# The seventh down chunk of both feed-forward networks by seven block products, with its fold spread over GpSimd and VectorE, in a two-block transformer kernel

## What is computed

```
def first_block(x, ...):
    ...
    h = rms_norm(x, norm_mlp[l])
    x = x + jnp.square(jax.nn.relu(h @ w_up[l])) @ w_down[l]
    return rms_norm(x, norm_final)

def second_block(x, ...):
    ...
    n2 = rms_norm_2(h, norm_mlp_pre[l])
    hid = jnp.square(jax.nn.relu(jnp.einsum('bsd,df->bsf', n2, w_up[l])))
    mlp_out = jnp.einsum('bsf,fd->bsd', hid, w_down[l])
    h = h + rms_norm_2(mlp_out, norm_mlp_post[l])
```

## Time and profile before

| | |
|---|---|
| median of 3 runs | 1567.17 us (1567.06 to 1567.26) |
| the profiled execution's own time | 1567.51 us |
| span from its first to its last instruction | 1565.7 us |
| TensorE busy | 1549.0 us, 99% of the span |
| VectorE, ScalarE, GpSimd busy | 987.3, 662.7, 482.6 us |
| down6 / down7 of the first network on TensorE | from 717.07 us / from 738.83 us |
| down6 / down7 of the second network on TensorE | from 1515.58 us / from 1537.34 us |

### The profile page before, as it was taken

The page is one execution under the profiler, slowest core; times in us unless marked ns, Lnnn a source line. Parts: engine busy times, 40 slices in busy tenths (PEclk is TensorE's granted clock), DMA queues, the critical chain, the costliest instruction groups (busy, mean ns, idle before and its releaser), DMA issues.

```text
span 1565.7 us, 21038 instructions
## 1 busy us (share of the span) xinstructions
PE 1549.0 (99%) x7752; PEld 1303.1 (83%) x7752; DVE 987.3 (63%) x1188; ACT 662.7 (42%) x1092; POOL 482.6 (31%) x282
## 2 busy tenths in 40 slices
PE   8999999999999999999999999999999999999998
PEld 6888888888788888888888898988888988888886
DVE  5454876435477776876664747357356677777765
ACT  5352665244444443443533433643334453434342
POOL 2451000000037776752300000020013047767732
PEclk9999999999999999999999999999999999999999
DMA  6422136221313233215332132243334332213133
GB/s 247 150 70 79 41 108 191 79 81 54 135 54 108 108 108 107 107 55 160 89 106 83 55 95 71 92 162 105 111 124 147 135 108 102 89 45 135 67 116 120
DMA packets 44997, 164.35 MB, mean 105 GB/s; under 512 B 5584, under 2 KB 5784, under 8 KB 44272
## 3 DMA queue, kind: packets, MB, share of 16 engines
q1 hardware_dynamic: 40608, 144.82, 28.4%
q0 software_dynamic: 4304, 18.38, 3.4%
HBM read 158.89 MB, written 5.85 MB: 105 GB/s over the span
## 4 chain that ended last, share of the span: by engine, by line
PE 93%; DVE 4%; ACT 2%; DMA 1%; issue 1%; SPq 0%; DVEq 0%; ACTq 0%
PE banks L1235 29%; PE banks L1237 29%; PE banks L1236 29%; PE banks L1534 1%; PE banks L1413 1%; DVE nmax L2230 1%; DVE w_lo L1944 1%; DMA w_raw<-in_weights 1%; PE banks L1352 0%; PE banks L1596 0%; DVE banks L2229 0%; PE banks L1572 0%; PE banks L1564 0%; PE banks L1523 0%; DMA x_tok<-in_x 0%
## 5 line engine op out<-in xcount | busy, mean ns | idle before, releaser
L1235 PE MATMUL banks<-act_hi,w_hi 128*128 128x512 f32 (+1 forms) x1088 | 413.7, 380 | 3.1 <-DVE act_lo L2112 3.1
L1237 PE MATMUL banks<-act_hi,w_lo 128*128 128x512 f32 (+1 forms) x1088 | 410.3, 377 | 0.0
L1236 PE MATMUL banks<-act_lo,w_hi 128*128 128x512 f32 (+1 forms) x1088 | 410.2, 377 | 0.0
L1944 DVE TENSOR_TENSOR w_lo<-w_raw,w_hi 128x1024 fp32r<-128x1024 f32 x216 | 280.0, 1303 | 203.2 <-ACT w_hi L1632 199.8
L1632 ACT ACTIVATE w_hi<-w_raw 128x1024 fp32r<-128x1024 f32 x216 | 227.0, 1059 | 251.6 <-DMA w_raw<-in_weights 196.8
L1235 PEld LDWEIGHTS banks<-act_hi,w_hi 128*128 128x128 f32 x1088 | 204.9, 188 | 40.8 <-DVE w_lo L1944 1.6
L1237 PEld LDWEIGHTS banks<-act_hi,w_lo 128*128 128x128 f32 x1088 | 204.9, 188 | 37.7
L1236 PEld LDWEIGHTS banks<-act_lo,w_hi 128*128 128x128 f32 x1088 | 205.0, 188 | 36.4
L1235 PE MATMUL banks<-w_hi,a_hi 128*128 128x512 f32 x400 | 155.8, 389 | 0.0
L1237 PE MATMUL banks<-w_hi,a_lo 128*128 128x512 f32 x400 | 155.7, 389 | 0.0
L1236 PE MATMUL banks<-w_lo,a_hi 128*128 128x512 f32 x400 | 155.7, 389 | 0.0
(11 more groups left out here) (367 smaller groups left out, 2393.4 us busy)
## 6 DMA issues: line engine op xcount, KB each, us to landing
w_raw<-in_weights SPq DMA_DIRECT2D x216, 512.0 KB, 3.7
w_down<-in_weights SPq DMA_DIRECT2D x48, 512.0 KB, 6.4
wide<-share_dram POOLq DMA_DIRECT2D x3, 1024.0 KB, 10.2
x_tok<-in_x SPq DMA_DIRECT2D x4, 512.0 KB, 5.2
w_first<-in_weights SPq DMA_DIRECT2D x4, 512.0 KB, 8.5
x_tok<-in_x POOLq DMA_DIRECT2D x4, 512.0 KB, 5.0
x_dram<-x_tok POOLq DMA_DIRECT2D x1, 2048.0 KB, 8.1
x_tok<-x_dram POOLq DMA_DIRECT2D x1, 2048.0 KB, 8.5
```

The lines of the kernel that those rows point to most:

```text
L1235: pe.matmul(out_ap, lhs[0], rhs[0], start=start, stop=False)
L1236: pe.matmul(out_ap, lhs[0], rhs[1], start=False, stop=False)
L1237: return pe.matmul(out_ap, lhs[1], rhs[0], start=False, stop=stop)
L1944: dve.tensor_tensor(w_lo[:, slot, :], landed(kind, raw), w_hi[:, slot, :], ALU.subtract).then_inc(lo_w, 1)
```

## The change

- `seven(g)` now takes in down6: its weights come through `w_down`, and `tsum` runs for it.
- `run_mlp` runs down6 as `s.products(dst, last=True)`. "whole" moves ahead of it, so GpSimd makes `act_lo` for down7 while down6 runs. The ScalarE and GpSimd work on the next chunk's parts, which a down step by products has otherwise, falls away there.
- `fold` leaves VectorE in up7. Its parts follow the products from which they can be made: after products 1, 2, 3 and 4 on GpSimd (`fold_on_pool`: six operations of 128x1024 in the first network, five in the second), after product 6 on VectorE (two operations, which wait for GpSimd's third and fourth). GpSimd waits for its own last one before it goes on, and the adds of down7 to the last quarter wait for it too.
- `load2` and `unpark` stand behind "whole" and ahead of the fold in GpSimd's order, and wait for product 0 to be read.
- The parked residual comes back into `x_late`, which lies over `w_down`, and the output is written from there.

```
-    return name in ("w_down", "w_down_2") and row0 < FF - 2 * T
+    return name in ("w_down", "w_down_2") and row0 < FF - T
...
+        if last:
+            sums, held = None, self.count("lo_a", 4)
+            self.add("whole", held=held, sq=squared)
...
-        s.add("whole", held=s.count("lo_a", 1), sq=s.count("sq", 0), dst="parts")
-        up(after="fold")
-        after_last()
-        steps = s.bank_steps("add", "tok", "parts", rows=4, halves=2, dst=dst)
-        go(steps, 1)
-        s.add("whole", held=s.count("lo_a", 4), sq=s.count("sq", 0), dst="act")
-        go(steps, 16)
-        s.add("unpark", ready=ready(), dst=dst)
+        up()
+        for st in s.products(dst, last=True):
+            taken = filled_by(st)
+            if st.n == 0:
+                after_last(taken)
+                s.add("unpark", ready=taken, dst=dst)
+            s.add("fold", n=st.n, ready=taken, dst=dst)
         last(s.bank_steps("add", "tok", "act", rows=4, halves=2, dst=dst, by_tile=True))
...
             def fold(st):
+                at_ = FOLDS[st.dst]
+                q, (x11, x12, x21, x22) = sums_of[st.dst], quarters(st.dst)
+                if st.n == 6:
+                    wait_ready(dve, st.ready, None)
+                    dve.wait_ge(fold_made, at_ + 3)
+                    dve.tensor_tensor(x12, x12, q["q1"], ALU.add)
+                    dve.wait_ge(fold_made, at_ + 4)
+                    then(dve.tensor_tensor(x21, x21, q["q7"], ALU.add))
...
+                    if st.rows == 4 and st.nth >= TT // 2 and st.half == 1:
+                        dve.wait_ge(fold_made, LAST_FOLD[st.dst])
...
-                    pool.dma_start(x[:].rearrange("q t d -> q (t d)"), x_dram).then_inc(x_again, 16)
+                    wait_ready(pool, st.ready, turn)
+                    pool.dma_start(x_late[:].rearrange("q t d -> q (t d)"), x_dram).then_inc(x_again, 16)
...
+            def fold_on_pool(st):
+                at_ = FOLDS[st.dst]
+                q, (x11, x12, x21, x22) = sums_of[st.dst], quarters(st.dst)
+                if st.n in (1, 2, 3, 4):
+                    wait_ready(pool, st.ready, None)
+                if st.n == 1:
+                    pool.tensor_tensor(x11, x11, q["q1"], ALU.add).then_inc(fold_made, 1)
+                elif st.n == 2:
+                    pool.tensor_tensor(q["q6"], q["q6"], q["q1"], ALU.add).then_inc(fold_made, 1)
+                    pool.wait_ge(fold_made, at_ + 2)
+                elif st.n == 3:
+                    pool.tensor_tensor(q["q1"], q["q6"], q["q5"], ALU.add).then_inc(fold_made, 1)
+                elif st.n == 4:
+                    pool.tensor_tensor(q["q7"], q["q7"], q["q6"], ALU.add).then_inc(fold_made, 1)
+                    pool.wait_ge(fold_made, at_ + 4)
+                    if st.dst == "y":
+                        pool.tensor_tensor(x22, q["q7"], q["q5"], ALU.add).then_inc(fold_made, 1)
+                    else:
+                        pool.tensor_tensor(q["q5"], q["q7"], q["q5"], ALU.add).then_inc(fold_made, 1)
+                        pool.wait_ge(fold_made, at_ + 5)
+                        pool.tensor_tensor(x22, x22, q["q5"], ALU.add).then_inc(fold_made, 1)
+                    pool.wait_ge(fold_made, LAST_FOLD[st.dst])
```

More of the change, by code:

```diff
@@ L374, in ahead, with products @@
         return out
-    def products(self, dst, first=False):
+    def products(self, dst, first=False, last=False):
         g = self.group
@@ L398, in products @@
             ends.append((bank + 1, self.cell(self.fills[bank + 1] + 1, ("bank", bank + 1))))
-            yield self.add("product", banks, n=j, dst=dst, first=first, splits=splits,
+            yield self.add("product", banks, n=j, dst=dst, first=first, last=last, splits=splits,
                            units=[self.placed(self.mine[j])], held=held, of=ends, sum_a=sums, sq=squared)
@@ L763, in make_schedule @@
     s.gemm("up", "T", "act", ready=act_ready, pairs=True)
-    run_mlp("x", lambda: s.add("load2", ready=all_out()), first_end)
+    run_mlp("x", lambda taken: s.add("load2", ready=taken), first_end)
     go(s.project0, 16)
@@ L1152, in part_lo, with quarters @@
             eng.tensor_tensor(a_lo[:, j], parts[j], a_hi[:, j], ALU.subtract).then_inc(lo_a, 1)
+        def quarters(dst):
+            rows_of = {"x": x, "y": y}[dst]
+            return [rows_of[:, 2 * rows:2 * rows + 2, 512 * cols_:512 * cols_ + 512] for rows in range(2) for cols_ in range(2)]
         def copies_of(st):
@@ L1967, in gemm @@
                     split(st, turn)
-                if st.after == "fold" and st.bank == 0:
-                    fold(st)
                 b = st.bank
@@ L2030, in handle @@
                     split(st, turn)
+                elif k == "fold":
+                    fold(st)
                 elif k == "product":
@@ L2400, in handle @@
                     block_sums(pool, st, turn)
-                elif k == "product":
+                elif k == "product" and not st.last:
                     for j in (st.n - 1, st.n) if st.n == 6 else (st.n - 1,):
```

62 lines of the change are left out of this document (22 added, 40 removed).

## The result

The changed kernel takes 1578.45 us (median of 6 runs, 1577.73 to 1585.32), the kernel before 1567.22 us beside it. The ratio over all these runs is 1.0078, 95% interval 1.0063 to 1.0094: slower by 0.8% (the two medians alone give 1.0072, or 11.2 us). The profiled execution took 1577.73 us, the shortest of the six, and 10.2 us more than that of before.

A forecast was written before the change was run, and what follows sets the result against it. TensorE, at work for 1549.0 of 1565.7 us, bounds the kernel. +6.9 (tile 0's chain), +2.0 (clock) and -0.6 (second network) give +8.3: 1575.8 us profiled, 1575.5 us as median, range 1570.0 to 1578.5.

The forecast's parts named there:

- they take turns, a whole instruction each: On the SBUF port shared by VectorE and GpSimd, each waits for one whole instruction of the other; 6.4 us on GpSimd's fold.
- the term of the second network: Second network: -2.72 us for the saved step, +2.1 us for product 6 waiting for a bank; -0.6 us, tail unchanged.
- What bounds the kernel: TensorE, at work for 1549.0 of 1565.7 us; only shortening its stream or making it wait moves the time.
- the step saved: Each down6 loses one of eight steps, 12 matmuls, 2.72 us; 5.4 us for both networks.
- The rival without port waits: No waits for the port at all: fold done at R 25.7, -4.4 us, 1562.8 us, faster; chance 0.07.
- The chain of tile 0: First network: fold, split, row product, factor and scaling start tile 0's transposes 40.2 us after down6 starts, against 33.3; +6.9 us.
- The wait for `h_tok`: First network: TensorE finishes tile 1, then stands idle once for 8 to 10 us ahead of tile 0's transposes.
- The clock: Idling 8 us brings TensorE to 1.2 GHz before tile 0's transposes in the first network; +2.0 us, bounds 0 and 5.4.
- VectorE has the room to catch up: Second network's down7: tile 0's adds at about R 27 come in time, so the tail keeps its length.

The follow-up runs named there:

- e7: The changed kernel with all fold operations left out on GpSimd and VectorE, so the output is not the reference's: 1563.59 us, ratio 0.9977.
- e9: First network as before the change; second by seven products, residual fetch behind the third fold operation, third and fourth splits behind the next add, x21 moved: 1565.02 us.
- e5: The changed kernel with the whole fold on GpSimd waiting for the add of product 4 instead of starting product by product: 1579.07 us, ratio 1.0074.
- e1: The changed kernel with one wait added: GpSimd's second fold operation first waits until its own first one is done: 1574.49 us, ratio 1.0046.
- e4: The changed kernel with three edits: own wait, weight splits behind the adds, fold of tiles 2 and 3 behind row products of tiles 0 and 1: 1571.23 us.
- e6: The changed kernel with the step making act_hi and act_lo behind product 0, so GpSimd's transfers stand ahead of the act_lo operations: 1580.63 us, ratio 1.0085.
- e8: First network as before the change; only the second has the seventh chunk by products, with its fold from the add of product 4 on: 1568.98 us.
- e2: The changed kernel with VectorE's third and fourth weight splits of the last down step by products behind the next product's add: 1574.46 us, ratio 1.0046.
- e3: The changed kernel, first network only: GpSimd's fold operations 4 to 6 behind row products of tiles 0 and 1, x21 ahead of tile 2's adds: 1581.19 us.

## Why the prediction was right in direction and too low

The sum said +8.3; the profiled execution gave +10.2 and the medians +11.2. The step that failed is the rule for the port, "they take turns, a whole instruction each", and through it the term of the second network, -0.6 forecast and +2.55 measured. By the prediction's own terms:

- **What bounds the kernel, and the step saved: right.** Both down6 have 84 matmuls; e7 and e9 give -2.6 and -2.7 for one network where nothing else is in the way. The rival without port waits, -4.4, is what e7, without any fold, comes near to (-3.6).
- **The chain of tile 0: right, +6.4 instead of +6.9.** The fold ended at R 30.1, and x21, which the forecast had ahead of the fold's end, at 31.2 (31.8 forecast for both); the split behind it ended at 32.4 (33.0), the row product at 34.5 (35.0), the factor at 37.9 (38.3), and the transposes started at 39.75 (40.2). The failed step below left this chain alone: the hold made VectorE wait, and GpSimd, on which the chain hangs, went on (2.44 and 2.36 us for its first two operations).
- **The wait for `h_tok`: 2.87 us instead of 8 to 10.** The time was lost earlier: TensorE stood 4.0 us ahead of product 6 and took 2.5 more for it at the lower clock, and the chain of tile 0 was as late as before for all that. In e5, with no product wait, it was 11.3.
- **"They take turns, a whole instruction each": this step failed.** It is true where the GpSimd instruction behind the running one has no transfer ahead of it (and e9), and it was carried over to a place that has transfers directly ahead. There the split waits for two fold operations. In the second network the times ahead of it came as forecast: fold operation 1 started at R 10.6 (10.8 forecast) and the third split asked at 11.4 (11.3), but it ended at 16.4 instead of 14.3, 5.04 us instead of 3.0. In the first network, where the forecast had the same wait or none, the fourth split took 5.52 us. The Trainium skill (SBUF — State Buffer, "SBUF: two separate sides") gives the pair to whoever starts first, for the whole instruction; the trace agrees that it is whole instructions, but e1 to e4 and e6 show splits that asked first and still came behind operations that had not begun, for up to 7.86 us.
- **Second network, -0.6 forecast, +2.55 measured: the term that broke the sum.** It is -2.72 for the step, +3.57 for product 5 (due at 1536.83, started at 1540.40; the forecast had product 6, 2.1 us), and +1.72 for the lower clock, since the last two products took 7.16 us where 24 warm matmuls take 5.44. The forecast had no clock cost there, because its wait was thought short.
- **The clock: the size right, the places not.** +1.6 us (T0 to T1, 7.97 against 6.41) instead of +2.0 behind `h_tok`; 2.2 in e5 behind the long wait. Unforeseen were the two falls in down6. The Trainium skill (TensorE: Matmul & The Clock Gate, "What's actually happening") says that the clock is low after idling and comes back with work; the trace agrees: 0.50 behind the waits, where the first transposes take 1.97 us, and full pace later, where those of tile 1 take 1.03.
- **"VectorE has the room to catch up": only with an early fold.** It holds in the changed kernel, where TensorE was late too, and not in e8, where the end of VectorE moved 3.1 us away from the last matmul.

The terms: +6.4 and +1.9 for the first network (the second of these is 1.6 at tile 1 and 0.3 behind it), +2.55, and -0.7 ahead of it all: +10.2.

The second network's loss is shown by e9 to be a matter of order: with one transfer, two weight splits and x21 each in a later place, the same fold on the same engines gives -2.7. Singly, the own wait gives -0.7 (e1) and the later splits -1.7 (e2). For the first network the runs show three causes: the hold behind seven transfers, a fold of 14.4 us on GpSimd in front of tile 0, and a port that has no room for it in down7 either. No order tried mends all three, and what each is worth alone was not measured. What stays open is by what GpSimd keeps the port. The hold does not cover the whole train of transfers either. A split that asked 1.60 us behind the start of the first of the seven was let in at once (727.98, changed kernel), and so was one at 1.68 us (722.98, e6); those at 1.70 to 1.75 us (e1, e2, e3, e4) were not. A version with the first network's fold on another path (VectorE, straight from the banks) wasn't tried.

## What to carry to other kernels

Work moved to GpSimd was paid here on VectorE wherever both read two operands from SBUF, and the price was not the mean of a share but whole instructions, two or more where GpSimd's operations follow its own transfers with their waits already met; put such transfers behind the operations, or a wait between. Ask of each VectorE instruction that may be held up what is queued behind it: an add that frees a bank should stand ahead of a split that nobody needs yet. And a step saved on TensorE is worth little where it ends in a chain that was already just late (1.1 of 2.7 us even without the fold, e7); work that is off the path in an earlier step should not be moved in front of that chain.

## What the runs showed of the hardware that I had not expected

- GpSimd's operations directly behind transfers that it issued itself, with nothing unmet to wait for, kept VectorE's two-operand instructions out until GpSimd next stood still: 5.52, 5.04 (changed kernel), 5.48 (e1), 7.86, 4.78 (e2), 7.77, 4.83 (e3), 5.54 (e4), 6.80, 7.43 us (e6) for a split of 1.2. In none of the 13 traces was any other VectorE instruction with its inputs in SBUF passed by a GpSimd operation that began more than 0.03 us after it had asked. A stop of 0.17 us was enough to let it in. Transfers alone did not (1.23 us in e5 and e7).
- TensorE's granted clock: behind waits of 1.10, 1.39, 1.54, 1.61, 1.81 and 1.97 us the matmuls went on at full pace; behind those of 2.87, 3.41, 3.72, 3.75, 4.22, 6.49 and 11.3 us they ran at 0.50 for a while, 0.43 us from start to start instead of 0.227. In the second network the first three after the wait of 3.41 us still went at full pace, and the fall came behind them.
- What a fall cost was 1.7 us and 2.5 us behind a bank wait, 1.6 us behind the wait of 2.87 us, and 2.2 us behind that of 11.3 us. It did not follow the length of the wait: 3.70 us (e1) cost 1.3, and 3.59 us (e6) 2.6.
